# Reordering the opening of a two-block transformer kernel: x ahead of the constants, constants issued by ScalarE, row sums on TensorE, columns inside a chunk

## The reference

```python
def rms_norm(x, g):
    xf = x.astype(jnp.float32)
    y = xf * lax.rsqrt(jnp.mean(xf * xf, axis=-1, keepdims=True) + RMS_EPS)
    return (y * g.astype(jnp.float32)).astype(x.dtype)
...
    sc = jax.nn.silu(c)
    scc = jax.nn.silu(c_ctx)
...
        mod = (sc @ w_mod[l] + b_mod[l])[:, None, :]
        sh1, sc1, g1, sh2, sc2, g2 = jnp.split(mod, N_MOD, axis=-1)
        u = modulate(rms_norm(h, norm1_g[l]), sh1, sc1)
...
            uc = modulate(rms_norm(hc, norm1_g[l]), csh1, csc1)
...
    p = u @ w_in
    kvc = uc @ w_in[:, FOUR_WIDTH + NA_WIDTH:]
```

## Time and profile before

| | |
|---|---|
| median of 3 runs | 1987.13 us (1984.03 to 1987.55) |
| span of the profiled execution, first to last instruction | 1985.5 us |
| PE busy | 1947.2 us, 98% |
| ACT, DVE, POOL busy | 683.5, 979.7, 923.2 us |
| HBM read | 217.55 MB, 111 GB/s over the span |
| mean granted clock of TensorE | 0.996 |

### The profile page before, as it was taken

One profiled execution on the slowest core, in us unless ns is written; L12 is line 12 of the kernel. 1 busy time (PEld: TensorE's weight loads), 2 busy tenths in 40 slices (PEclk: granted clock), 3 DMA queues, 4 the chain that ended last, 5 costly groups with the idle time before them and its releaser, 6 DMA issues. The chain is left out here.

```text
span 1985.5 us, 25740 instructions
## 1 busy us (share of the span) xinstructions
PE 1947.2 (98%) x10104; PEld 1600.5 (81%) x10104; DVE 979.7 (49%) x1472; ACT 683.5 (34%) x904; POOL 923.2 (46%) x699
## 2 busy tenths in 40 slices
PE   7999999999999999999999999999999999999998
PEld 6976778888888788888888767888888888888886
DVE  4667889593846451422334463376663453122123
ACT  4323733121222531222234454365554252212122
POOL 3334364555555434545464224444434555444444
PEclk9999999999999999999999999999999999999999
DMA  8563162643442413222223112212122222222211
GB/s 338 170 175 136 44 233 85 246 157 148 172 166 79 151 64 105 86 103 87 106 85 113 43 43 80 106 64 86 64 85 85 87 100 92 104 88 104 105 65 43
DMA packets 42782, 223.07 MB, mean 112 GB/s; under 512 B 12736, under 2 KB 13248, under 8 KB 17344
## 3 DMA queue, kind: packets, MB, share of 16 engines
q1 hardware_dynamic: 42688, 221.77, 30.8%
HBM read 217.55 MB, written 2.10 MB: 111 GB/s over the span
## 5 line engine op out<-in xcount | busy, mean ns | idle before, releaser
L1004 POOL TENSOR_TENSOR wl<-raw,wh 128x512 fp32r<-128x512 f32 x611 | 842.0, 1409 | 994.9 <-ACT wh L545 898.1
L1109 PE MATMUL bank<-uh,wh 128*128 128x512 f32 x1432 | 571.7, 399 | 2.2 <-POOL wl L1004 1.1
L1111 PE MATMUL bank<-uh,wl 128*128 128x512 f32 x1432 | 559.4, 391 | 0.0
L1110 PE MATMUL bank<-ul,wh 128*128 128x512 f32 x1432 | 558.9, 390 | 0.0
L545 ACT ACTIVATE wh<-raw 128x2048 fp32r<-128x2048 f32 (+1 forms) x149 | 281.2, 1888 | 567.4 <-PE bank L1111 558.3
L1109 PE MATMUL bank<-ah,wh 128*128 128x512 f32 x848 | 331.5, 391 | 0.0
L1111 PE MATMUL bank<-ah,wl 128*128 128x512 f32 x848 | 330.1, 389 | 0.0
L1110 PE MATMUL bank<-al,wh 128*128 128x512 f32 x848 | 330.1, 389 | 0.0
L1109 PEld LDWEIGHTS bank<-uh,wh 128*128 128x128 f32 x1432 | 269.5, 188 | 69.9 <-issue 10.9
L1110 PEld LDWEIGHTS bank<-ul,wh 128*128 128x128 f32 x1432 | 269.6, 188 | 57.0 <-issue 3.4
L1111 PEld LDWEIGHTS bank<-uh,wl 128*128 128x128 f32 x1432 | 269.3, 188 | 57.1
(11 more groups left out here) (272 smaller groups left out, 2073.4 us busy)
## 6 DMA issues: line engine op xcount, KB each, us to landing
raw<-in_w SPq DMA_DIRECT2D x64, 1024.0 KB, 4.8
mraw<-in_w_modr SPq DMA_DIRECT2D x36, 1024.0 KB, 4.8
raw<-in_w_gu SPq DMA_DIRECT2D x22, 1024.0 KB, 4.8
raw<-in_w_hg SPq DMA_DIRECT2D x16, 1024.0 KB, 4.8
raw<-in_w_in SPq DMA_DIRECT2D x8, 1024.0 KB, 9.7
modf<-in_w_modf SPq DMA_DIRECT2D x8, 1024.0 KB, 20.2
raw<-in_w_out SPq DMA_DIRECT2D x8, 1024.0 KB, 5.1
raw<-in_w_dn SPq DMA_DIRECT2D x8, 1024.0 KB, 4.8
```

The source lines that it names most:

```text
L1004: pool.tensor_tensor(wl[:, slot, c + k:c + k + 2], raw[:, b % RAW, k:k + 2], f32(wh[:, slot, c + k:c + k + 2]), ALU.subtract).then_inc(spl ...
L1109: pe.matmul(out, ah_, bh, start=first, stop=False)
L1110: pe.matmul(out, ah_, bl, start=False, stop=False)
L1111: return pe.matmul(out, al_, bh, start=False, stop=last)
```

## The change

Five things change, all in the opening. SP no longer issues `craw`, `con`, `vec` and `bmod`; ACT issues them as its first four instructions, and SP begins with x, then `modf[0]`, then weight block 0. The squares of x are no longer added on DVE: PE sums each one as it comes, in the form of rows (`rows`, four matmuls of 128x128 with 32 weight columns), with two `keep_clock` matmuls between, and root, reciprocal and spread work on a 128x128 tile `xrow` as those of the later norms do. ACT loads the table for the root early, by one element's root, and splits block 0 after the root. The `keep_clock` at the start goes from 30 to 14 and three more stand before the first columns. Last, `first_columns(k + 1)` is issued between the two halves of `chunk_products(0, k)`, and the chunks of block 1 are set between others.

```diff
-            sp.dma_start(craw[:], t["c_cols"]).then_inc(c_in, 16)
-            sp.dma_start(con[:, 0:C_END], t["consts"]).then_inc(const_in, 16)
-            sp.dma_start(vec[:, 0:V_END], t["vecs"]).then_inc(const_in, 16)
-            sp.dma_start(bmod[:], t["b_mod"]).then_inc(const_in, 16)
...
-            load(0, t["w_in"][0])
             for i in range(8):
                 sp.dma_start(modf[:, i], t["w_modf"][i]).then_inc(modf_in[i], 16)
+                if i == 0:
+                    load(0, t["w_in"][0])
...
+            act.dma_start(craw[:], t["c_cols"]).then_inc(c_in, 16)
+            act.dma_start(con[:, 0:C_END], t["consts"]).then_inc(const_in, 16)
+            act.dma_start(vec[:, 0:V_END], t["vecs"]).then_inc(const_in, 16)
+            act.dma_start(bmod[:], t["b_mod"]).then_inc(const_in, 16)
             act.wait_ge(c_in, 16)
             act.activation(csil[:], craw[:], ACT.Silu).then_inc(csil_ready, 1)
             act.wait_ge(const_in, 48)
+            act.activation(rc[:, 0, 0:1], eps_col, ACT.Sqrt)
             for k in range(KC):
                 h_wait(act, "x", k)
                 act.activation(sqx[:, k, :], h[:, k, :], ACT.Square).then_inc(sq_ready, 1)
-            split(0)
             root("x")
...
             rows_out(0)
+            split(0)
...
             def sum_x():
-                pe.wait_ge(x_added, KC - 1)
-                for a in range(S // P):
-                    last = pe.matmul(bank[6][:, a:a + 1], sqx[:, KC - 1, P * a:P * a + P], ones_v[:, 0:1], start=(a == 0), stop=(a == S // P - 1), skip_group_check=True)
+                for k in range(KC):
+                    pe.wait_ge(sq_ready, k + 1)
+                    last = rows(bank[6], sqx[:, k], k == 0, k == KC - 1)
+                    if k < KC - 1:
+                        keep_clock(2)
...
+                    if columns is not None and half == 0:
+                        first_columns(columns)
...
-            keep_clock(30)
+            keep_clock(14)
             pe.wait_ge(csilp_ready, 1)
             sum_x()
             first_rows(0)
+            keep_clock(3)
+            first_columns(0)
             norm_spread("x")
-            first_columns(0)
             first_rows(1)
-            first_columns(1)
-            for u in (2, 3, 4):
-                first_rows(u)
-                chunk_products(0, u - 2)
-                first_columns(u)
...
+            for u in range(1, 5):
+                chunk_products(0, u - 1, u)
+                first_rows(u + 1)
+            for u in (5, 6, 7):
+                chunk_products(1, u - 5)
+                chunk_products(0, u - 1, u)
+                if u < KC - 1:
+                    first_rows(u + 1)
+            chunk_products(1, 3)
             sum_ctx()
-            chunk_products(1, 3)
+            chunk_products(0, 7)
             norm_spread("ctx", L)
-            for b, k in ((0, 7), (1, 4), (1, 5), (1, 6), (1, 7)):
-                chunk_products(b, k)
+            for k in range(4, KC):
+                chunk_products(1, k)
```

More of the change, by code:

```diff
@@ L136, in build_program @@
         rrow = at("rrow", [P, 2, P], F32, A + 74 * KB)
+        xrow = at("xrow", [P, 2, P], F32, A + 73 * KB)
         ah = at("ah", [P, KC, S], F32R, A)
@@ L202, in build_program @@
         macc, mcol_full, mcol_used = sem("macc"), sem("mcol_full"), sem("mcol_used")
-        csil_ready, csilp_zero, csilp_ready, x_added, c_added, rows_full, rows_copied, mod0_full, mod0_ready, gx_ready = (
-            sem("csil_ready"), sem("csilp_zero"), sem("csilp_ready"), sem("x_added"), sem("c_added"), sem("rows_full"), sem("rows_copied"),
+        csil_ready, csilp_zero, csilp_ready, c_added, rows_full, rows_copied, mod0_full, mod0_ready, gx_ready = (
+            sem("csil_ready"), sem("csilp_zero"), sem("csilp_ready"), sem("c_added"), sem("rows_full"), sem("rows_copied"),
             sem("mod0_full"), sem("mod0_ready"), sem("gx_ready"))
@@ L331, in norm_sqs, with norm_row @@
             return sqs0 if name == "ctx" else sqs1
+        def norm_row(name):
+            return xrow if name == "x" else rrow
         def norm_banks(name):
@@ L575, in root @@
                 act.wait_ge(sum_full, i + 1)
-                out, c = (rrow[:, 0, :], P) if name not in ("x", "ctx") else (rc[:, 0, 0:n // P], n // P)
+                out, c = (norm_row(name)[:, 0, :], P) if name != "ctx" else (rc[:, 0, 0:n // P], n // P)
                 act.activation(out, norm_banks(name)[0][:, 0:c], ACT.Sqrt, bias=eps_col, scale=P / D).then_inc(root_ready, 1)
@@ L1192, in norm_spread @@
                 for a in range(n // P):
-                    if name not in ("x", "ctx"):
-                        last = pe.matmul(rms[:, P * a:P * a + P], ident[:, 32 * a:32 * a + 1].to_broadcast([P, P]), rrow[:, 1, :], start=True, stop=True)
+                    if name != "ctx":
+                        last = pe.matmul(rms[:, P * a:P * a + P], ident[:, 32 * a:32 * a + 1].to_broadcast([P, P]), norm_row(name)[:, 1, :], start=True, stop=True)
                     else:
@@ L1201, in normalise @@
                 norm_sum(name, n)
-                if name not in ("x", "ctx"):
-                    keep_clock(2)
+                keep_clock(2)
                 norm_spread(name, n)
-                if name not in ("x", "ctx"):
-                    keep_clock(8)
+                keep_clock(8)
             def first_product(name, b):
@@ L1258, in first_columns, with chunk_products @@
                 last.then_inc(mod0_full, 1)
-            def chunk_products(b, k):
+            def chunk_products(b, k, columns=None):
                 pe.wait_ge(split_lo, lows(b, k // 2 + 1))
@@ L1713, in norm_factor @@
                     dve.wait_ge(rms_full, i)
-                if name not in ("x", "ctx"):
-                    dve.reciprocal(rrow[:, 1, :], rrow[:, 0, :]).then_inc(rstd_ready, 1)
+                if name != "ctx":
+                    dve.reciprocal(norm_row(name)[:, 1, :], norm_row(name)[:, 0, :]).then_inc(rstd_ready, 1)
                 else:
@@ L1813, in _ @@
             dve.tensor_copy(csilp[:, :, 0:2], csil[:]).then_inc(csilp_ready, 1)
[L1814 to L1818, removed]
             norm_factor("x")
```

## The result

The changed kernel takes 2003.16 us in the median of its runs, the kernel before 1987.34: a ratio of 1.0081 with a 95% interval of 1.0067 to 1.0095, so 0.8% slower. One of the changed kernel's four runs, in which the clock of TensorE stayed at 0.556, is left out of the ratio, though not of the median; the other three took 2001.35 to 2003.93. The forecast was 1994.5 within 1986.4 to 1998.5: the sign was right, the size (7.4 us) was about half of the measured one (0.81%, 16.1 us), and the range missed it.

A forecast was written before the change was run, and what follows sets the result against it. PE was taken as the bound from 60 us, so its start decides: +6.0 us up to the first `tt`, +3.25 in the chunks, -1.8 at the context, +7.4 on 1987.1, giving 1994.5; range 1986.4 to 1998.5.

The forecast's parts named there:

- The mark and how it carries on: PE's first product with the context, at 60.94 us: x us later there makes the end about x us later.
- I take c = 12: Opening: last constant assumed to land at 12 us, near the upper end, making the first `tt` 6.0 us later.
- c: Time the last constant lands, which PE's first instruction waits for; 5.4 us before, bounds 3.8 to 13.9.
- the upper case: Constants' landing: two queues take turns, one constant per 1 MB transfer; 13.9 us, or 11.4 with ACT's queue first.
- From c to the first `tt`: Opening, behind the last constant: clock matmuls, sums, rows, columns and spread on PE's queue, 13.8 us in all.
- The step between two sums: Row sums of x on PE: four matmuls 0.30 plus two clock matmuls 0.46, 0.76 us, times seven 5.3.
- The eight chunks: From the first `tt` to the end of the last `ul`: 32.6 us against 29.34, +3.25 us.
- The loop of 4.1 us: First four chunk steps: columns inside a product that waits for `ul` close a ring through DVE and PE, 4.1 us each.
- worth nothing more: Opening: dropped DVE adds and `split(0)` behind the root bring no further gain, since PE's queue replaces their path.
- the low stretch: Kernel before, 22.13 to 25.54 us: granted clock at 0.51, costing up to 1.7 us within the chunks' 29.34.
- The context: From the last `ul` to the context's products: 9.97 us against 11.80, -1.8 us, PE waiting some 2 us for `ucl`.
- a fall of the clock: Eight chunks after the change: a possible drop of the granted clock, 0 to 1.7 us, counted only in the range.

The follow-up runs named there:

- e1: Changed kernel with the four constants issued by SP ahead of x again; ratio 1.0034 to the kernel before.
- e2: Kernel before with only the four constants moved from SP's queue to ACT's; ratio 1.0036 to the kernel before.
- e3: Changed kernel with `con`, `vec` and `bmod` packed into one transfer on ACT's queue; ratio 1.0048 to the kernel before.
- e9: Changed kernel with the transfer of `con` on ACT's queue cut into two by columns; ratio 1.0096 to the kernel before.
- e7: Changed kernel with constants on SP ahead of x and the old order of rows, chunks and columns; ratio 1.0011 to the kernel before.
- e10: Changed kernel with `split(0)` ahead of the root on ACT again; ratio 1.0064 to the kernel before.
- e4: Changed kernel without the two clock matmuls between the row sums; ratio 1.0057 to the kernel before.
- e6: Kernel before with only PE's order of rows, chunks and columns changed to the new one; ratio 1.0025 to the kernel before.

## Why the prediction was right in sign and wrong in size

**The mark and how it carries on: right.** The loss at the context's start (14.5) is the loss of the span (14.1), within 0.4 us.

**The step that failed: "I take c = 12", and its bound of 13.9.** c was 14.63, which is 2.6 us of the 7.1 that are missing. The mechanism was the upper case, the two queues in turn, and e1, e2, e3 and e9 show it. I had priced that case at 13.9, or 11.4 if ACT's queue has the first turn, and then taken 12: 1.9 of the 2.6 us are this choice, for which no row had a figure. The other 0.7 is the price itself, which let the first 1 MB land after the time of a lone transfer and the others follow at 2.5 us; measured are 6.0 for the first and 3.2, 2.8 and 2.6 for the three behind it. With 8 rows for each DMA engine in every transfer of both queues, each constant lasts about as long as one 1 MB transfer.

The Trainium skill (DMA: Bandwidth & Descriptors, Queues, rings and completion order) says that an engine goes round-robin between the queues and takes a packet at a turn, typically 9 to 17 descriptors. The trace agrees with the round-robin. With the unit it agrees only if what the profile counts as a packet is not one descriptor: 50 packets of one queue stand beside 51 of the other within 1 us. No run here shows which it is.

**From c to the first `tt`: 13.8 forecast, 16.07 measured.** The step between two sums was priced at 0.76 and took 1.00 (20.10 to 21.10): 1.7 us over seven steps. The 14 clock matmuls at the start took 5.5 instead of 4.7. More of them took the longer of the two times in the earlier trace rows than I reckoned; the granted clock reads 1.00 over all of them, and the same 14 took 4.74 us in e7 and 6.29 in e10, so this part is scatter between executions. e4 shows that this queue of PE's, and not ACT's squares, was the path.

**The eight chunks: 32.6 forecast, 34.67 measured.** The loop of 4.1 us was right: from `tt` to `tt` 4.16 for the second and third step, and 4.70 for the fourth against 4.8. The first took 5.48, and e10 shows why: `split(0)` behind the root makes POOL late, so that it works beside DVE, and DVE's `ul` and `gm` are slow beside it. That is the cost of an edit which I had put at nothing ("worth nothing more"). The steps five to seven took 4.85, 4.76 and 4.27 against 4.4; in the fifth, a `ul` beside POOL took 1.44 us. Two readings in this piece were loose without weight: a whole product is 2.95 - 1.0 - 0.5 = 1.45, not 1.43, and ahead of the low stretch PE had not done little but was busy for 2.14 of 3.40 us (18.7 to 22.1).

**The context: 9.97 forecast, 10.04 measured,** with PE waiting 2.03 us for `ucl`, as said.

The three misses are 2.6 + 2.3 + 2.1 = 7.0 us, all one way, and they are the difference between 7.4 and 14.5. The range had been built from the bounds of c and 1.7 us for a fall of the clock; the price of a sum's step and that of the chunks had no bounds. A fourth miss shows against the runs, not against the profile: the 29.34 us that I took for the chunks before have the low stretch in them, and e2 takes 27.81. That adds 1.5 us to the loss, and 16.0 is what the runs show (16.1).

By parts, the runs put the queue alone at 0.36% (e2), the columns alone at 0.25% (e6) and all the rest at 0.11% (e7): 0.72% together, against 0.81% for the whole. The intervals, some 0.1% to either side of each, don't tell the two apart. One place where the parts don't simply add stands in the profiles: 9.1 us of c cost the kernel before 6.7 us at the first `tt` (e2), and 9.3 us cost the changed order 9.2 (e1), since there nothing hides the wait for c.

## What to carry to other kernels

Small constants that the first instructions of several engines wait for belong ahead of the bulk in the same queue, or in one packed transfer; a second queue beside a full one makes them late by their count of rows. When work for the next round is set behind an instruction that waits for this round's result, follow the waits round once: if they form a ring, its length is the time of a step. Count matmuls that keep the clock as work, as soon as they stand on the path. And before a single profile is taken as the base of a sum of a few us, look for stretches of low clock in it.

## What the runs showed of the hardware

Transfers of 8 to 195 KB on one queue, beside 1 MB transfers on another, landed 2.6 to 3.2 us apart; the same four had all landed at 5.4 us when they stood first in one queue. A DVE `ul` of 0.75 us and a `gm` of 0.16 took 1.51 and 0.73 beside a POOL subtraction of 128x512 float32, while a `tt` of 0.75 and an `mx` of 0.16, which read a PSUM bank, kept their times beside it. Executions of one kernel differ with the share of low clock that they get: the five of e10 have mean clocks of 0.993 to 0.999 and spans of 2003.8 to 1995.5 us, the longest at the lowest clock.
